# Weight casts moved ahead of shifted copies, a turned bonus between two gate products, ten unread transposes and seven semaphore clears fewer, in an RWKV/attention/MoE kernel

## What is computed

```python
xs = h[None] + xx[None] * mu[:, None, None, :]
r, k, v = jnp.einsum('pbtd,pde->pbte', xs[:3], w_rkv)      # three 1024 x 1024 products
w = -jax.nn.softplus(-(w0 + jnp.tanh(xw @ w1) @ w2)) - 0.5  # decay
a = jax.nn.sigmoid(a0 + (xa @ a1) @ a2)
g = jax.nn.sigmoid(xg @ g1) @ g2                            # the gate
_, y = lax.scan(_rwkv7_step, S0, (r, decay, k, v, -kk, kk * a))
bonus = jnp.sum(rh * kh * r_k.astype(f32), -1, keepdims=True) * vh
out = (yn + bonus.reshape(B, T, D)).astype(h.dtype) * g
```

## Time and profile before

| | |
|---|---|
| median of 3 runs | 2842.15 us (2839.92 to 2848.01) |
| profiled execution | 2859.77 us, of which its span is 2858.0 us |
| PE busy | 2611.4 us (91% of the span) |
| DVE busy | 2057.1 us (72%) |
| ACT busy | 980.9 us (34%) |
| POOL busy | 393.1 us (14%) |
| mean granted TensorE clock | 0.951 |

### The profile page before, as it was taken

The page is one execution under the profiler, slowest core; times in us unless marked ns, Lnnn a source line. Parts: engine busy times, 40 slices in busy tenths (PEclk is TensorE's granted clock), DMA queues, the critical chain, the costliest instruction groups (busy, mean ns, idle before and its releaser), DMA issues. The chain is left out here.

```text
span 2858.0 us, 43183 instructions
## 1 busy us (share of the span) xinstructions
PE 2611.4 (91%) x17344; PEld 2030.7 (71%) x17344; DVE 2057.1 (72%) x2802; ACT 980.9 (34%) x1056; POOL 393.1 (14%) x210
## 2 busy tenths in 40 slices
PE   5899888788999989998899996999898999999993
PEld 3674788546888854574788885897667788888882
DVE  6772576788777547645877757785865799999994
ACT  2531111122221013332122103333321677777772
POOL 1000000100000001000000000000001266666651
PEclk8998999999999989999999998999898999999997
DMA  5220222316664262201566422331216699999973
GB/s 194 77 81 10 82 91 77 134 52 191 180 190 138 96 212 95 74 31 51 178 187 180 147 96 95 96 97 59 105 43 232 220 369 370 375 368 364 362 303 133
DMA packets 247812, 459.65 MB, mean 161 GB/s; under 512 B 31125, under 2 KB 205869, under 8 KB 232313
## 3 DMA queue, kind: packets, MB, share of 16 engines
q1 hardware_dynamic: 227736, 433.74, 43.7%
q0 software_dynamic: 14256, 23.72, 2.4%
q10 hardware_dynamic: 5682, 0.20, 0.1%
HBM read 457.09 MB, written 30.56 MB: 171 GB/s over the span
## 5 line engine op out<-in xcount | busy, mean ns | idle before, releaser
L49 PE MATMUL ffn_bank<-ffn_xT_high,ffn_wi_high 128*128 128x512 f32 x704 | 279.6, 397 | 10.1 <-DVE ffn_wi_low L43 5.7
L50 PE MATMUL ffn_bank<-ffn_xT_low,ffn_wi_high 128*128 128x512 f32 x704 | 277.9, 395 | 0.0
L409 DVE SCALAR_TENSOR_TENSOR ffn_nsum<-ffn_nw,ffn_cond,ffn_nsum 128x256 f32<-128x256 f32 x336 | 163.0, 485 | 12.0
L49 PEld LDWEIGHTS ffn_bank<-ffn_xT_high,ffn_wi_high 128*128 128x128 f32 x704 | 133.7, 190 | 41.2 <-DVE ffn_wi_low L43 6.6
L3202 POOL DMA_INDIRECT expert_rows<-exp_ys,exp_to_row x32 | 155.9, 4871 | 45.1 <-issue 44.3
L50 PEld LDWEIGHTS ffn_bank<-ffn_xT_low,ffn_wi_high 128*128 128x128 f32 x704 | 133.4, 189 | 28.4
L43 DVE TENSOR_TENSOR moe_u_low<-moe_u,exp_u_high 128x4096 fp32r<-128x4096 f32 x32 | 141.6, 4425 | 13.5 <-ACT exp_u_high L3276 13.4
L43 DVE TENSOR_TENSOR moe_g_low<-moe_g,moe_g_high 128x4096 fp32r<-128x4096 f32 x32 | 141.7, 4428 | 9.3 <-ACT moe_g_high L3276 9.1
L49 PE MATMUL ffn_bank<-ffn_wo_high,ffn_act_high 128*128 128x512 f32 x352 | 138.6, 394 | 5.3 <-DVE ffn_wo_low L43 5.3
L43 DVE TENSOR_TENSOR moe_d_low<-moe_d,exp_d_high 128x4096 fp32r<-128x4096 f32 x32 | 141.4, 4418 | 0.0
L51 PE MATMUL ffn_bank<-ffn_xT_high,ffn_wi_low 128*128 128x512 f32 x352 | 139.5, 396 | 0.0
(11 more groups left out here) (690 smaller groups left out, 6585.4 us busy)
## 6 DMA issues: line engine op xcount, KB each, us to landing
moe_g<-in_w_e_gate SPq DMA_DIRECT2D x32, 2048.0 KB, 9.2
moe_u<-in_w_e_up SPq DMA_DIRECT2D x32, 2048.0 KB, 9.2
moe_d<-in_w_e_down SPq DMA_DIRECT2D x32, 2048.0 KB, 9.1
ffn_nw<-in_ada_w SPq DMA_DIRECT2D x24, 1024.0 KB
ffn_nw<-in_w_ada SPq DMA_DIRECT2D x24, 1024.0 KB
stay_z<-in_ffn_w_in SPq DMA_DIRECT2D x44, 512.0 KB, 5.2
ffn_wi<-in_ffn_w_in SPq DMA_DIRECT2D x44, 512.0 KB, 5.2
ffn_wo<-in_ffn_w_out SPq DMA_DIRECT2D x44, 512.0 KB, 3.5
```

The source lines that it names most:

```text
L49: nc.tensor.matmul(out, w[0], x[0], start=start, stop=False, **kw)
L50: nc.tensor.matmul(out, w[0], x[1], start=False, stop=False, **kw)
L409: nc.vector.scalar_tensor_tensor(out=total, in0=nw[:, b, k, :], scalar=cond[:, k:k + 1], in1=total, op0=ALU.mult, op1=ALU.add).then_inc(s[ ...
```

## The change

- `quarter_high(2)` on ACT moves to after slice 1's factors and ahead of `shift(0)`; `quarter_high(3)` to after `shift(4)`. `quarter_low(2)` on DVE moves ahead of the whole loop over slices, `quarter_low(3)` to after slice 6.
- The bonus is turned after Hg0, between the gate's two first products. After Hg1 PE does ten unread transposes.
- The masks are loaded in proj by POOL, once `h_done` has reached 8, into a tile that lives through the whole time mix; chunks waits for that load.
- `Room.clear` keeps a list of used semaphores and clears only after mixed, ffn0, ffn1 and hyb, then all that have gathered. The clears after proj, chunks, dsa, route, exp, comb and moe go, with their two barriers each; the barrier at the end of each block stays.

```diff
+USED = []
+CLEARED_AFTER = ("mixed", "ffn0", "ffn1", "hyb")
...
     def clear(self):
-        if self.sems:
+        USED.extend(self.sems)
+        if self.sems and self.phase in CLEARED_AFTER:
             self.nc.all_engine_barrier()
-            self.nc.clear_and_free_semaphores(self.sems)
+            self.nc.clear_and_free_semaphores(USED)
             self.nc.all_engine_barrier()
+            USED.clear()
...
             pool.dma_start(head_rows_raw, head_rows_dram).then_inc(selector_loaded, 16)
+            pool.wait_ge(h_done, KD)
+            pool.dma_start(buf["masks"][:, :, :], masks_dram).then_inc(buf["masks_loaded"], 16)
...
-                if (name, q) == ("G", 0):
+                if (name, q) == ("Hg", 1):
+                    keep_busy(nc, bank[4], ident, 10)
+                if (name, q) == ("Hg", 0):
                     pe.wait_ge(bonus_done, 1)
                     for t in range(NT):
                         last = nc.tensor.transpose(bank[7][:, t * HEADS:(t + 1) * HEADS], bonus[:, t * P:(t + 1) * P], ident[0:HEADS, 0:HEADS])
...
+                if q == 1:
+                    quarter_high(2)
                 if q:
                     shift(q - 1)
                 if q == 5:
-                    quarter_high(2)
+                    quarter_high(3)
             shift(KD - 1)
-            quarter_high(3)
...
+            quarter_low(2)
             for q in range(KD):
                 dve.wait_ge(exps_done, q + 1)
...
                 if 0 < q < 4:
                     receptance(q - 1)
-                if q == 5:
-                    quarter_low(2)
+                if q == 6:
+                    quarter_low(3)
             for q in range(3, KD - 1):
                 receptance(q)
                 if q == 3:
                     for k in range(KD):
                         mix_one(V_xs, 1, k)
-                if q == 4:
-                    quarter_low(3)
                 if q == 6:
                     quarter_low(4)
...
-            sp.dma_start(masks[:, :, :], masks_dram).then_inc(s["loaded"], 16)
...
-            pe.wait_ge(s["loaded"], 16)
+            pe.wait_ge(buf["masks_loaded"], 16)
...
-            dve.wait_ge(s["loaded"], 16)
+            dve.wait_ge(buf["masks_loaded"], 16)
```

More of the change, by code:

```diff
@@ L491, with rwkv_project @@
 HALF_P = P // 2
-def rwkv_project(nc, room, buf, stay, x_in, cond_in, ada_w, ada_b, w, ident_dram, head_rows_dram):
+def rwkv_project(nc, room, buf, stay, x_in, cond_in, ada_w, ada_b, w, ident_dram, head_rows_dram, masks_dram):
     AR, BT, KT, V, G, PC, BON, cond = (buf[n] for n in ("AR", "BT", "KT", "V", "G", "PC", "BON", "cond"))
@@ L1028, in rwkv_buffers @@
         "BON": room.sb("BON", [P, NT, HEADS]), "cond": room.sb("cond", [P, KD]),
+        "masks": room.sb("masks", [P, LEVELS + 4, CHUNK]), "masks_loaded": room.sem("masks_loaded"),
     }
@@ L1053, in head_rows, with rwkv_chunks @@
     return np.repeat(np.eye(HEADS, dtype=np.float32), HD, axis=1)
-def rwkv_chunks(nc, room, buf, Y, acc, stay, ada_w, ada_b, masks_dram):
+def rwkv_chunks(nc, room, buf, Y, acc, stay, ada_w, ada_b):
     AR, BT, KT, V, PC, cond = (buf[n] for n in ("AR", "BT", "KT", "V", "PC", "cond"))
@@ L1069, in head @@
         return slice((2 * q + e) * HD, (2 * q + e + 1) * HD)
-    masks = room.sb("masks", [P, LEVELS + 4, CHUNK])
+    masks = buf["masks"]
     ident = stay["ident"]
@@ L1083, in rwkv_chunks @@
     pA, pB, pC, pD = (room.ps(n, [P, 2, HALF]) for n in ("pA", "pB", "pC", "pD"))
-    names = """loaded s_zeroed tr_psum tr_done l_psum x0_done b_psum b_read lt_done rb_done k_psum mk_done w_psum w_done x_psum x_done
+    names = """s_zeroed tr_psum tr_done l_psum x0_done b_psum b_read lt_done rb_done k_psum mk_done w_psum w_done x_psum x_done
                z_psum z_done ut_psum ut_done rg_psum rg_done own_psum gs_psum s_done y_psum y_done steps
@@ L1548, in rwkv @@
         with ExitStack() as inner:
-            rwkv_project(nc, Room(nc, inner, "proj"), buf, stay, x_in, cond_in, ada_w, ada_b, w, ident_dram, head_rows_dram)
+            rwkv_project(nc, Room(nc, inner, "proj"), buf, stay, x_in, cond_in, ada_w, ada_b, w, ident_dram, head_rows_dram, masks_dram)
         Y = Room(nc, ctx, "rwkv").sb("Y", [P, NT, D])
@@ L1552, in rwkv @@
         with ExitStack() as inner:
-            rwkv_chunks(nc, Room(nc, inner, "chunks"), buf, Y, acc, stay, ada_w, ada_b, masks_dram)
+            rwkv_chunks(nc, Room(nc, inner, "chunks"), buf, Y, acc, stay, ada_w, ada_b)
         with ExitStack() as inner:
```

## The result

| | before | changed |
|---|---|---|
| median, first comparison | 2841.91 us (6 executions) | 2828.02 us (6), 2824.13 to 2832.37 |
| ratio, 95% interval | | 0.9949, 0.9935 to 0.9963 |
| profiled execution, its span | 2859.77, 2858.0 us | 2824.13, 2822.4 us |
| PE busy | 2611.4 us | 2589.0 us |
| mean granted TensorE clock | 0.951 | 0.964 |

The median fell by 13.9 us where 17.0 were forecast, and the ratio's interval allows 10.5 to 18.5; 2828.0 lies inside the range of 2807 to 2834. The two profiled executions lie 35.6 us apart. Some 13 us of that are the clock at the gate, which the profiled execution of before had at half and most executions of it did not, as the experiments show.

A forecast was written before the change was run, and what follows sets the result against it. PE bounds the kernel, busy 91% of the span, so edits pay where it idles, runs at half clock or all engines stand. 6.5 + 0 - 0.1 + 4.4 + 1.5 + 4.7 = 17.0 off 2842.15 gives 2825.1 us, range 2807 to 2834.

The forecast's parts named there:

- Casts: Proj: stall before R4 goes, a new 2.4 us one comes before R6, K0 starts at about 122.7; 6.5 us gained.
- The cold stretch after R6: Proj: half-clock matmuls behind the new stall may cost 0 to 2.7 us; 1 taken.
- Gate: End of proj: timed runs already had a warm gate, so the edit saves 0.0 in the median, bounds 0 and 14.1.
- The 14.1: G1 to G7: us saved if 14 products take 1.0 each at full clock instead of 2.0.
- Case B: Gate: timed runs had it cold like the profiled one and the change mends it; 31.1 saved, 2811.0; chance 0.25.
- The delay of G0 by the unread transposes: Gate: transposes put behind Hg1 can hold G0 up by 0 to 0.15 us; 0.1 taken.
- From proj to chunks: Start of chunks: PE starts with the block, 4.4 us saved (1.1 clear, 3.3 masks), plus 1.5 from transposes at full clock.
- the 1.5: Start of chunks: us saved if first transposes run at full clock, given a warm gate; bounds 0 and 1.6.
- The other clears: Phase ends besides proj's: six clears removed save 5.8, deferred range clears cost 1.0; net 4.7, bounds 4.0 and 5.8.
- C: Proj: the stall before R6 is longer than counted, casts give 0; 10.5 saved, 2831.6; chance 0.08.
- D: Gate: transposes don't hold the clock, which falls after the change; 1.4 saved, 2840.7; chance 0.08.
- E: Proj: clock falls at the new stall before R6 and stays at half; slower, 2872; chance 0.04.

The follow-up runs named there:

- casts alone: Only the four moves of the casts and low parts, against the kernel before: median 2837.0 us (12 executions), ratio 0.9966.
- the changed kernel again: The changed kernel, unchanged, run and profiled a second time, against the kernel before: median 2825.7 us (6 executions), ratio 0.9934.
- clears alone: Four semaphore clears instead of eleven; masks, casts and gate as in the kernel before: median 2838.0 us (11 executions), ratio 0.9984.
- The parts' medians: Casts' moves, gate edits, and masks with clears, each put singly into the kernel before: medians 2837.0, 2840.4 and 2834.7 us.
- the pair of longer idle times: The kernel before with four more sigmoids ahead of G0: 2858.8 us; the same with thirty unread transposes behind Hg1: 2842.4 us.

## Why the prediction was right

**Casts.** The hand-made schedule held within 0.5 us at each point: `quarter_low(3)` to 109.2 (109.6), R6 at 109.37 (109.7), K0 at 122.18 (122.7), the cause DVE's `x_low`, as named. The 7.1 us at K0 lie just above the bounds of 5 to 7. The cold stretch after R6, taken at 1 us, is itself a matter of chance: of the four profiled executions with this stall it came in two (casts alone, the changed kernel again) and not in the other two (the clock was 1.00 from 109 to 114 in the changed kernel's first profile). It costs nothing at K0 in either case (122.17 with it, 122.18 without), for DVE is later than PE; so the term had no bearing on K0 at all. In proj the part is worth 7, and that DVE sets K0 was shown by taking its work off the path (118.20). In the median casts alone gave 4.9. The forecast took a gain at K0 to be a gain at the end; for 2 us of it (2.8 against the lower group) that wasn't seen, and why stays open.

**Gate.** The choice of 0 for the median was the step on which the number hung, and its reason held: the profiled execution of before was one of a minority. The 17.6 us between it and the median was the right hint (the groups lie 18.3 apart). The 14.1 was a little large: with the products at 1.05 us each rather than 1.0, proj ends 13.3 sooner. Case B has fallen. But "nothing in the median" isn't nothing: one execution in seven was 18 us longer, which is 2.7 in the mean. The delay of G0 by the unread transposes was taken at 0.1 and is 0.3: the prediction read 256.75 as the end of Hg1, where the view has the start of its last product (its end is at 257.3).

**From proj to chunks.** 4.45 to 0.1 us and 5.91 to 4.36, as worked out (4.4 and 1.5), and the clear's share of 1.1 was seen by itself. The prediction tied the 1.5 to a warm gate and left open whether the wait for the masks cools the clock by itself. It does. In the second profile of the kernel before the clock was at 1.00 to the end of the gate and fell while PE waited (a window as in the earlier trace rows, and PE's first work in chunks):

```profile
278.00:280.00 2.00, 0.00 (x0) 0.00 (x0) 0.00 (x0) 0.00 (x0) 2.00 (x1) 0.50 0.86 291
280.32 1.97 PE L1138 MATMUL chunks_pA<-stay_ident,rwkv_BT 128*128 128x128 f32 x8 [5.13 <-DMA chunks_masks<-in_masks]
```

In all nine profiled executions that wait for the masks in chunks, seven of them with a warm gate, the first eight transposes took 1.97 us, and the second products stood 5.4 to 6.6 us behind them (5.96 in the mean); in all five with the masks loaded in proj it was 1.06 and 4.4. So the 1.6 us came with the load of the masks, not with the gate.

**The other clears.** Here the sum was too large. Six clears less are worth 5.8, as taken; the 1.5 of them behind comb are seen to be gone. But the four that are left take 6.0 us from the block's release to the clear's instead of 4.2: 1.8 more, where 1.0 was taken. The range clears themselves make only 0.7 of that (0.63 instead of 0.15 at mixed, 0.52 instead of 0.26 at ffn1). Most of the rest lies at ffn0, where the two range clears are as long as before but start 0.7 us apart instead of 0.2; why isn't shown. The net is 4.0, the lower of the prediction's bounds, instead of 4.7. In time the 5.8 of clears alone, with proj's own, is compatible with the run (3.8, interval -1 to 10), not confirmed by it.

**Sum.** The terms as the traces show them are 7.1 for the casts, -0.3 for G0's delay, 4.4 and 1.6 from proj to chunks and 4.0 for the other clears: 16.8, against 17.0 forecast. So near a sum is luck in part, for the casts came out larger and the clears smaller. The measured gain is 13.9 in the first comparison and 15.0 with more executions, about 2 either way, so the 1.8 that are missing lie within the error. The parts' medians, 4.9, 1.6 and 7.3, make 13.8. If something is missing, it may be in stretches at half clock that shift from execution to execution (the phase mixed took 89.1 us in one profiled execution of the kernel before and 92.5 in the other; the phase hyb 410.2 to 415.4 in the eight profiles with the clears as before, 410.9 to 416.2 in the six with four). The runs can't place it.

**The rivals.** C (the wait only moves) fell with K0 at 122.18. D (transposes don't hold the clock) fell with the pair of longer idle times, 2858.8 against 2842.4. E named a fall at R6 that stays. The fall did come in two of four profiled executions; what didn't come is that it stays: behind some 3 us the clock was back at 1.00. Its reason, 38 us at half clock "with PE busy", counted in the 5.47 us in which PE waits for the masks. Still, a fall that stays is real at another place: the idle time of 3.24 us in front of G0 did cost the whole gate, and the kernel with it was slower than before. Why the clock comes back within some 3 us at R6 and not in the gate wasn't tried.

## What to carry to other kernels

A single profiled execution can show a stretch at half clock that most executions don't have: before an edit is credited with it, set the profiled time against the median, or profile the kernel a second time. Idle time on PE costs little by itself and much if the clock falls behind it; unread transposes in it keep the clock up (thirty in 3.24 us, shown) and cost little (ten in 0.77 us delayed the next product by 0.3). Where a stall has been removed, read what is next on the path (here DVE's list), for the same reordering done once more gave another 4 us.

## What was not expected of the hardware

An idle time of 3.24 us instead of 0.77 in front of G0 turned a fall of the clock that came in 15 of 103 executions into one in five of five (one of them profiled, the others by their times), and PE didn't get the full clock back in 30 us of uninterrupted products (0.50 from 264 to 292), while at R4, after 8 us of idle time, it came back in 6, and at R6, after 2.5, in some 3 where it fell at all. A stall of 8 us cost 2.7 us in clock, one of 3 us about 15 (proj's end in the pair of profiles, less their difference of 1.0 at Hg0): what a stall costs isn't read from its length. What sets them apart, the work behind the stall or something else, stays open.
